# A hybrid decoder layer in split float32 on one core: memory keys in wide and narrow matmuls, a bank per 128 features, and another order of the small products around them

## The chip, the cores and the metric

One NeuronCore of a Trainium2 chip runs the whole layer as one program. The metric is the device time of one execution in microseconds, median of several runs. TensorE is called PE here (its weight loads PEld), VectorE DVE, ScalarE ACT, GpSimd POOL and SyncE SP.

## What is computed

```python
# x, mem: (1, 256, 1024) float32, one layer
proj = h @ w_in                       # qa ka va | qg kg vg rg glr
moba_o = causal softmax attention, 8 heads x 64, ALiBi     # one block of 256: plain causal
b = cumsum(log_sigmoid(glr @ w_gate_up + b_gate) / 16)     # gated linear attention, 4 heads
attn = einsum('bhtd,bhsd,bhtsd->bhts', qg, kg, exp(b_t - b_s))   # causal, chunks of 64
gla_o = rmsnorm(attn @ vg + carried state) * gla_norm_g * silu(rg)
x = LN1(alpha*x + concat(moba_o, gla_o) @ w_mix_o)
k, v = split(mem @ w_xkv)             # 4 heads x 256, 256 memory tokens
x = LN2(alpha*x + softmax((x @ w_xq) k^T / 16) v @ w_xo)
x = LN3(alpha*x + relu(x @ w_ff1)**2 @ w_ff2)
```

## The kernel before

Every large matmul is done in three parts: each float32 operand is split into a high part (rounded to `float32r`) and a low part, and hi x hi, hi x lo and lo x hi are added up in a bank of PSUM. Weights come in units of 128x2048 (half a "chunk" of 512 columns or 512 rows) into four raw buffers. ACT casts a unit to `w_hi` (`hi_half`), DVE subtracts to get `w_lo` (`lo_half`), and only then can PE use the low part and SP load the unit four places on. Both weight tensors have two places, taken by the chunk's parity. There are no queues with a scheduler: each engine's instructions stand in the order in which its block is written, and they are tied by counting semaphores. `FRONT_FILLS` says which bank each result takes and how often the bank has been filled before, `CHUNK_END` which result must be full before a chunk's weight buffer is overwritten.

The part that matters here lies between the softmax of the self attention and the mixing projection. The names in PE's program:

- `pt0` to `pt7`: transposes of the eight heads' probabilities. `rg0`, `rg1`: the gate of the linear attention. `pv0`, `pv1`: probabilities times values, four heads each. `diag`: the diagonal of the linear attention, 4 tiny float32 matmuls.
- `xk0` to `xk3`: memory keys, one bank for 256 features, made by `features`: two groups of 128 features, each 8 steps of three 128x256 matmuls (`three`). The activations (the transposed memory) are in `actB_hi` and `actB_lo`.
- `lv0` to `lv6` and `off0`, `off1`: the decayed products of the linear attention, one level for each distance 64, 32, ..., 1. For each level DVE makes exponents (`exponents`), ACT exponentiates (`decay`), POOL multiplies keys and queries by them, PE multiplies (`level`, float32, 128x128 x4), and DVE puts the result into `att` under a mask (`masked`). `off` is the product between chunks.
- `xv00`, `xv01`: memory values by `tokens` (8 steps of three 128x512 matmuls). `av0`, `av1`: `att` times the values. `mo00` to `mo11`: the mixing projection, chunk 9 and then chunk 10 by `rows`; in the last quarter of chunk 9 stand `gt0`, `gt1`, the transposes of the gated result.

Behind `av` there is a chain of engines: DVE adds the diagonal (L1090), ACT squares (L703), DVE and POOL make the scale, DVE applies it (L1103), makes the low half of chunk 10's first unit (L891), and, once ACT has copied the transposes (L651), their low parts (L1050) and the low half of the second unit. `rows(10, ...)` on PE wants the latter at its third step of 12 (k = 2). The low half of chunk 9's second unit is made by DVE ahead of `av`, from a cast that stands on ACT's list behind the two copies of `off0` and `off1` (L693).

The query projection of the cross attention, later in the kernel, already has another form (`block`, with `high` and `low`): a bank holds 128 features in two halves. One 128x512 matmul of the high weights runs over high and low activations side by side, and one 128x256 matmul of the low weights adds to the right half. The halves are added afterwards.

Of the kernel before, what the change touches and what calls it, by code (L numbers as in the profile page):

```python
# [109 lines left out]
def raw_count(u):  # L110
# [25 lines left out]
CHUNK_END = {0: "kg1", 1: "qa3", 2: "ka3", 3: "va1", 4: "vg1", 5: "rg1", 6: "xk1", 7: "xk3", 8: "xv01",  # L136
# [5 lines left out]
def build(nc, x, xT, memT, w_in, w_glr, w_gate_up, b_gate, gla_norm_g, w_mix_o, ln1_g, ln1_b, w_xq, w_xkv,  # L142
# [7 lines left out]
    with ctx:  # L150
        def sb(name, shape, dt=f32):
            return ctx.enter_context(nc.sbuf_tensor(name, shape, dt))

        def sem(name):
            return ctx.enter_context(nc.semaphore(name))
# [8 lines left out]
        actB_hi = sb("actB_hi", [P, 8, S], f32r)  # L164
        actB_lo = sb("actB_lo", [P, 8, S], f32r)
# [65 lines left out]
        lng = probs[:, 2048:3072]  # L231
        memv = probsT[:, 0:2048].rearrange("p (t n) -> p t n", t=2)
# [68 lines left out]
        mem_hi, mem_lo = sem("mem_hi"), sem("mem_lo")  # L301
# [231 lines left out]
        def _(act):  # L533
# [12 lines left out]
            def hi_half(c, half):  # L546
                hi(unit(c, half), w_hi[:, c % 2, half, :], c)
# [92 lines left out]
            for h in range(4, 8):  # L640
                transposed(h)
            hi_half(6, 1)
# [11 lines left out]
            mix(1, "pv1")  # L654
            b = wait_full(act, "diag")
            act.copy(diag[:], b[:, 0:8]).then_inc(freed("diag"), 1)
# [9 lines left out]
            def memk(n):  # L666
                evacuate(f"xk{n}", memkT[:, 2 * n:2 * n + 2, :].rearrange("p m s -> p (m s)"))
# [16 lines left out]
            decay(7)  # L684
            act.wait_ge(x_in, 16)
            for c in range(2):
                wait_out(act, f"xk{2 + c}")
                seed(bank[FILL[f"mo0{c}"][0]], 0, c)
            hi_half(9, 0)
# [22 lines left out]
            def piece(k, name=None):  # L712
                if name is None:
                    wait_full(act, "av1")
                    wait_out(act, "lv6")
                    src = mem_pieces[k]
# [163 lines left out]
        def _(dve):  # L880
# [177 lines left out]
            lo_half(6, 1)  # L1058
            silu(1)
            mix(0, "pv0")  # L1060
            mix(1, "pv1")
# [3 lines left out]
            lo_half(7, 1)  # L1065
            masked(0)
            exponents(4)
            masked(1)
            lo_half(8, 0)
            exponents(5)  # L1070
            masked(2)
            lo_half(8, 1)
            exponents(6)
            masked(3)
            exponents(7)
            masked(4)
# [251 lines left out]
        def _(pe):  # L1328
# [7 lines left out]
            def full(name):  # L1336
                return bank_full[FILL[name][0]]
# [75 lines left out]
            def high(c, dst, k, m):  # L1413

                pe.matmul(dst[:, :].rearrange("p (h s) -> p h s", h=2), weight(c, k, m * P, (m + 1) * P)[0],  # L1415
                          actA[:, :, k, :], start=k == 0, stop=False, skip_group_check=True)

            def low(c, dst, k, m):
                return pe.matmul(dst[:, S:2 * S], weight(c, k, m * P, (m + 1) * P)[1], actA_hi[:, k, :],  # L1419
                                 start=False, stop=k == 7, skip_group_check=True)  # L1420
# [90 lines left out]

            tokens(3, 0, A, "va0")
# [12 lines left out]
            for h in range(4, 8):  # L1525
                transpose_probs(h)
            tokens(5, 1, A, "rg1")
            for name in ["va0", "va1"] + [f"pt{h}" for h in range(HA)]:
                wait_out(pe, name)
            for n in range(2):  # L1530
                b = begin(f"pv{n}")
                for h in range(4 * n, 4 * n + 4):
                    r = slice(64 * (h % 2), 64 * (h % 2) + 64)
                    c = (h // 2 - 2 * n) * S
                    pe.matmul(b[r, c:c + S], va[:, 0, h * DA:(h + 1) * DA], probsT[:, h * 384:h * 384 + S],  # L1535
                              start=True, stop=False)
                    i = pe.matmul(b[r, c + P:c + S], va[:, 1, h * DA:(h + 1) * DA],
                                  probsT[:, h * 384 + S:h * 384 + 384], start=False, stop=True)
                i.then_inc(full(f"pv{n}"), 1)
            b = begin("diag")  # L1540
            pe.wait_ge(qkdiag_done, 1)
            pe.wait_ge(headsel_done, 2)
            for t in range(2):
                for f in range(2):
                    k = 4 * t + 2 * f
                    i = pe.matmul(b[:, k:k + 2], qkdiag[:, f * S + t * P:f * S + (t + 1) * P], headsel[:],
                                  start=True, stop=True)
            i.then_inc(full("diag"), 1)

# [242 lines left out]
```

## Time and profile before

| | us |
|---|---|
| median of 3 runs | 408.29 |
| range of the runs | 408.09 to 408.89 |
| profiled execution, its own time | 407.74 |
| its span, first to last instruction | 405.9 |

The page gives busy shares by engine, and the chain that ended last: followed back from the last instruction, it says in which engine's hands the time lay. A matmul's duration in the timeline overlaps that of the next, since they are pipelined; what one costs is read from the distance of starts. A float32 matmul shows as two entries (4 matmuls are "x8"), a `float32r` one as one.

### The profile page before, as it was taken

Reading aid. Unit: us, or ns where it says so; the run is one execution under the profiler, and the core shown is the slowest. Engines: PE = TensorE matmul, PEld = TensorE weight load, DVE = VectorE, ACT = ScalarE, POOL = GpSimd, SP = SyncE. Lnnn points to the kernel's source line nnn. Section 1 sums busy time; section 2 is a strip of 40 time slices with the busy share of each in tenths; the row PEclk is TensorE's granted clock in tenths of the full one; section 3 lists DMA queues with packets and bytes.
Section 4 is the critical chain, followed back from the end, with each engine's and each line's share of the span. In section 5 each row is a group of like instructions: output and inputs, shape, how many; then the busy total and the mean of one; then the engine's idle time right before and its main releaser. Section 6 shows DMA issues by size and latency. Waiting matters only on the chain.

```text
span 405.9 us, 5774 instructions
## 1 busy us (share of the span) xinstructions
PE 398.2 (98%) x2208; PEld 343.1 (85%) x2208; DVE 280.7 (69%) x364; ACT 206.3 (51%) x286; POOL 63.6 (16%) x61
## 2 busy tenths in 40 slices
PE   8999999999999999999999999999999999999993
PEld 5888888899988888899988888888888888888882
DVE  4689566998784796968658859383746475664826
ACT  6666569656264628555733466352716343444400
POOL 2039400046950105000006100000000000000000
PEclk9999999999999999999999999999999999999999
DMA  8998737635526390837265274645665637364002
GB/s 282 314 393 290 259 117 290 222 105 208 207 105 207 107 304 6 286 130 221 92 206 178 54 288 146 207 175 200 207 208 182 231 111 269 136 220 194 0 0 103
DMA packets 32364, 75.70 MB, mean 186 GB/s; under 512 B 1526, under 2 KB 3926, under 8 KB 32342
## 3 DMA queue, kind: packets, MB, share of 16 engines
q1 hardware_dynamic: 31952, 75.24, 53.6%
q10 hardware_dynamic: 390, 0.17, 0.3%
q8 instruction: 14, 0.23, 0.2%
q14 instruction: 8, 0.07, 0.0%
HBM read 74.35 MB, written 1.05 MB: 186 GB/s over the span
## 4 chain that ended last, share of the span: by engine, by line
PE 98%; DVE 1%; issue 0%; POOL 0%; DVEq 0%; POOLq 0%
PE bank L1341 20%; PE bank L1342 19%; PE bank L1343 19%; PE bank L1729 13%; PE bank L1415 8%; PE bank L1734 7%; PE bank L1419 4%; PE bank L1557 2%; PE bank L1347 1%; PE bank L1407 1%; PE bank L1509 1%; PE bank L1535 0%; PE bank L1590 0%; PE bank L1642 0%; PE bank L1501 0%; PE bank L1500 0%
## 5 line engine op out<-in xcount | busy, mean ns | idle before, releaser
L891 DVE TENSOR_TENSOR w_lo<-raw,w_hi 128x2048 fp32r<-128x2048 f32 x36 | 83.8, 2334 | 13.4 <-ACT w_hi L544 13.3
L1276 DVE TENSOR_TENSOR w_lo<-raw,w_hi 128x2048 fp32r<-128x2048 f32 x24 | 55.0, 2291 | 40.3 <-ACT w_hi L828 40.3
L544 ACT CAST w_hi<-raw 128x2048 fp32r<-128x2048 f32 x38 | 72.2, 1917 | 18.1 <-PE bank L1343 14.2
L1341 PE MATMUL bank<-w_hi,actB_hi 128*128 128x512 f32 x192 | 75.6, 394 | 0.0
L1342 PE MATMUL bank<-w_lo,actB_hi 128*128 128x512 f32 x192 | 74.8, 390 | 0.0
L1343 PE MATMUL bank<-w_hi,actB_lo 128*128 128x512 f32 x192 | 74.8, 389 | 0.0
L828 ACT CAST w_hi<-raw 128x2048 fp32r<-128x2048 f32 x24 | 46.0, 1916 | 38.2 <-PE bank L1343 38.2
L1729 PE MATMUL bank<-actA,w_hi 128*128 128x512 f32 x224 | 53.3, 390 | 0.0
L1729 PEld LDWEIGHTS bank<-actA,w_hi 128*128 128x128 f32 x224 | 41.6, 188 | 8.3
L1343 PEld LDWEIGHTS bank<-w_hi,actB_lo 128*128 128x128 f32 x192 | 36.0, 188 | 7.6
L1341 PEld LDWEIGHTS bank<-w_hi,actB_hi 128*128 128x128 f32 x192 | 36.1, 188 | 7.2
L1342 PEld LDWEIGHTS bank<-w_lo,actB_hi 128*128 128x128 f32 x192 | 36.1, 188 | 6.9
L1341 PE MATMUL bank<-w_hi,actA 128*128 128x512 f32 x96 | 38.2, 397 | 0.0
L1343 PE MATMUL bank<-w_hi,actA 128*128 128x512 f32 x96 | 37.5, 390 | 0.0
L1342 PE MATMUL bank<-w_lo,actA 128*128 128x512 f32 x96 | 37.4, 390 | 0.0
L1415 PE MATMUL bank<-actA,w_hi 128*128 128x512 f32 x144 | 35.9, 392 | 0.0
L520 POOL TENSOR_TENSOR rstd<-vareps,minus_half 128x1 f32<-128x1 f32 x6 | 3.3, 545 | 194.9 <-DVE vareps L1122 194.8
L1415 PEld LDWEIGHTS bank<-actA,w_hi 128*128 128x128 f32 x144 | 26.0, 188 | 5.4 <-issue 0.7
L1734 PEld LDWEIGHTS bank<-actA,w_lo 128*128 128x128 f32 x224 | 28.7, 191 | 1.1
L1734 PE MATMUL bank<-actA,w_lo 128*128 128x256 f32 x224 | 29.1, 283 | 0.0
L813 ACT COPY att<-bank 128x256 f32<-128x256 f32 x28 | 10.3, 377 | 34.5 <-PE bank L1734 34.5
L1341 PEld LDWEIGHTS bank<-w_hi,actA 128*128 128x128 f32 x96 | 18.0, 188 | 4.4 <-issue 0.7
(192 smaller groups left out, 617.4 us busy)
## 6 DMA issues: line engine op xcount, KB each, us to landing
raw<-in_w_ff SPq DMA_DIRECT2D x32, 1024.0 KB, 5.3
raw<-in_w_in SPq DMA_DIRECT2D x10, 1024.0 KB, 7.9
raw<-in_w_xkv SPq DMA_DIRECT2D x8, 1024.0 KB, 5.0
raw<-in_w_mix_o SPq DMA_DIRECT2D x4, 1024.0 KB, 4.9
raw<-in_w_xq SPq DMA_DIRECT2D x4, 1024.0 KB, 5.1
raw<-in_w_xo SPq DMA_DIRECT2D x4, 1024.0 KB, 4.9
raw<-in_w_in SPq DMA_DIRECT2D x4, 512.0 KB, 5.6
probs<-in_ln_g SPq DMA_DIRECT2D x3, 512.0 KB, 6.2
```

What stands on the lines that cost most here:

```text
L544: act.copy(dst, half_view(u)).then_inc(hi_done, 1)
L813: act.copy(relu[:, f, m * S:(m + 1) * S], bank[b][:, S:2 * S]).then_inc(small_done, 1)
L828: act.copy(w_hi[:, (C_LOOP + k) % 2, half, :], raw[:, u % RAW, :]).then_inc(hi_done, 1)
L891: dve.tensor_tensor(dst, half_view(u), hi_part.bitcast(f32), ALU.subtract).then_inc(lo_done, 1)
L1276: dve.tensor_tensor(w_lo[:, c % 2, half, :], raw[:, u % RAW, :], w_hi[:, c % 2, half, :].bitcast(f32), ALU.subtract).then_inc(lo_done, 1)
L1341: pe.matmul(dst, stat[0], mov[0], start=start, stop=False, skip_group_check=on)
L1342: pe.matmul(dst, stat[0], mov[1], start=False, stop=False, skip_group_check=on)
L1343: return pe.matmul(dst, stat[1], mov[0], start=False, stop=stop, skip_group_check=on)
L1415: pe.matmul(dst[:, :].rearrange("p (h s) -> p h s", h=2), weight(c, k, m * P, (m + 1) * P)[0], actA[:, :, k, :], start=k == 0, stop=False, ...
L1419: return pe.matmul(dst[:, S:2 * S], weight(c, k, m * P, (m + 1) * P)[1], actA_hi[:, k, :], start=False, stop=k == 7, skip_group_check=True)
L1729: pe.matmul(bank[m][:, :].rearrange("p (h s) -> p h s", h=2), w_hi[:, par, k // 4, a:a + P], actA[:, :, k, :], start=k == 0, stop=False, s ...
L1734: i = pe.matmul(bank[m][:, S:2 * S], w_lo[:, par, k // 4, a:a + P], actA_hi[:, k, :], start=False, stop=k == 7, skip_group_check=True)
```

## The change

The memory keys get the form of `block`: eight results `xk00` to `xk31` of 128 features, a bank each, by `high` and `low` over `actB` (now one tensor with both parts). ACT copies both halves of each bank to SBUF (`memk`, eight copies of 128x512 where there were four), and DVE adds the halves (`memk_sum`, five additions with both operands in SBUF) behind the low half of chunk 9's second unit and ahead of the diagonal. `diag` and `pv0` move ahead of `rg1`, right behind the transposes; `pv1` goes behind `xk10`. The levels are done two at a time, the last with `off`; level pairs 4, 5 and 6, `off` stand in the middle of `xv00` and `xv01`. On ACT and DVE the copies, exponents and half conversions are put in an order that follows this.

```diff
@@ FRONT_FILLS, CHUNK_END
-    + [("rg1", 3), ("pv0", 4), ("pv1", 5), ("diag", 6), ("xk0", 0), ("xk1", 1)]
-    + [("lv0", 4), ("lv1", 5), ("xk2", 2), ("lv2", 6), ("lv3", 7), ("xk3", 3), ("lv4", 4), ("lv5", 5),
-       ("xv00", 0), ("lv6", 6), ("off0", 7), ("off1", 4), ("xv01", 1), ("av0", 5), ("av1", 6)]
+    + [("diag", 0), ("pv0", 1), ("rg1", 3), ("xk00", 0), ("xk01", 1)]
+    + [("xk10", 2), ("pv1", 7), ("lv0", 4), ("lv1", 5), ("xk11", 3), ("xk20", 0), ("xk21", 1), ("xk30", 2),
+       ("lv2", 6), ("lv3", 7), ("xk31", 3),
+       ("xv00", 0), ("lv4", 4), ("lv5", 5), ("xv01", 1), ("lv6", 6), ("off0", 7), ("off1", 4), ("av0", 5), ("av1", 6)]
@@ ACT
+            def memk(h, m):
+                evacuate(f"xk{h}{m}", memk_halves[h][:, m].rearrange("p h s -> p (h s)"))
             decay(0)
             hi_half(7, 0)
             decay(1)
-            memk(0)
+            memk(0, 0)
             hi_half(7, 1)
+            memk(0, 1)
+            memk(1, 0)
+            mix(1, "pv1")
             decay(2)
             decay(3)
-            memk(1)
+            memk(1, 1)
             hi_half(8, 0)
+            memk(2, 0)
+            hi_half(8, 1)
+            memk(2, 1)
+            memk(3, 0)
             decay(4)
-            hi_half(8, 1)
-            memk(2)
             decay(5)
+            memk(3, 1)
             decay(6)
-            memk(3)
+            hi_half(9, 0)
             decay(7)
@@ DVE
             masked(6)
-            lo_half(9, 0)
             lo_half(9, 1)
+            def memk_sum(h):
+                wait_out(dve, f"xk{h}1")
+                parts = [(0, 1), (1, 2)] if h == 0 else [(0, 2)]
+                for a, b in parts:
+                    v = memk_halves[h][:, a:b]
+                    i = dve.tensor_tensor(memkT[:, 2 * h + a:2 * h + b, :], v[:, :, 0, :], v[:, :, 1, :], ALU.add)
+                    if b < 2:
+                        link(i)
+                i.then_inc(mem_sum, 1)
+            memk_sum(0)
+            for h in range(1, HX):
+                dve.wait_ge(mem_sum, h)
+                memk_sum(h)
             wait_out(dve, "diag")
@@ PE
-            features(6, 0, B, "xk0")
-            features(6, 1, B, "xk1", between=lambda: level(0))
-            level(1)
-            features(7, 0, B, "xk2", between=lambda: level(2))
-            level(3)
-            features(7, 1, B, "xk3", between=lambda: level(4))
-            level(5)
-            tokens(8, 0, B, "xv00", between={4: lambda: level(6)})
-            off()
-            tokens(8, 1, B, "xv01")
+            memory_keys(0, 0)
+            memory_keys(0, 1)
+            memory_keys(1, 0)
+            values_of(1)
+            level(0)
+            level(1)
+            memory_keys(1, 1)
+            memory_keys(2, 0)
+            memory_keys(2, 1)
+            memory_keys(3, 0)
+            level(2)
+            level(3)
+            memory_keys(3, 1)
+            tokens(8, 0, B, "xv00", between={4: levels_4_5})
+            tokens(8, 1, B, "xv01", between={4: last_level})
```

Where the order moves, first on PE around the first memory keys. Before, the second group of `xk1` (bank 1) has the first level (bank 4) between its groups:

```order
L1341 MATMUL bank1<-actB_hi,w_hi 128x256
L1342 MATMUL bank1<-actB_lo,w_hi 128x256
L1343 MATMUL bank1<-actB_hi,w_lo 128x256
L1557 MATMUL bank4<-reset,qk 128x128 [waits bank_free4,lev_done]
L1557 MATMUL bank4<-reset,qk 128x128 x3
L1341 MATMUL bank1<-actB_hi,w_hi 128x256
L1342 MATMUL bank1<-actB_lo,w_hi 128x256
L1343 MATMUL bank1<-actB_hi,w_lo 128x256
```

and now `xk10` (bank 2) is followed by `pv1` (bank 7), whose first and last rows are shown, and by the levels 0 and 1 (banks 4 and 5), and then by `xk11` (bank 3):

```order
L1439 MATMUL bank2<-actB,w_hi 128x512 [waits bank_free2]
L1439 MATMUL bank2<-actB,w_hi 128x512 x7
L1443 MATMUL bank2<-actB,w_lo 128x256 x8
L1543 MATMUL bank7<-probsT,values 64x256 [waits bank_free6,bank_free5,bank_free7,bank_free4]
...
L1545 MATMUL bank7<-probsT,values 64x128
L1586 MATMUL bank4<-reset,qk 128x128 [waits bank_free4,lev_done]
L1586 MATMUL bank4<-reset,qk 128x128 x3
L1586 MATMUL bank5<-qkdiag,qk 128x128 [waits bank_free5,lev_done]
L1586 MATMUL bank5<-qkdiag,qk 128x128 x3
L1439 MATMUL bank3<-actB,w_hi 128x512 [waits bank_free3]
L1439 MATMUL bank3<-actB,w_hi 128x512 x7
L1443 MATMUL bank3<-actB,w_lo 128x256 x8
```

Three matmuls a step have become two, one of them of 512 columns, and three small products stand together.

Second, on PE in the memory values. Before, level 6 (bank 6) stands in the middle of `xv00` (bank 0), and `off` (banks 7 and 4) between it and `xv01` (bank 1):

```order
L1342 MATMUL bank0<-w_lo,actB_hi 128x512
L1343 MATMUL bank0<-w_hi,actB_lo 128x512
L1557 MATMUL bank6<-reset,qk 128x128 [waits bank_free6,lev_done,lo_done]
L1557 MATMUL bank6<-reset,qk 128x128 x3
L1341 MATMUL bank0<-w_hi,actB_hi 128x512
...
L1343 MATMUL bank0<-w_hi,actB_lo 128x512
L1568 MATMUL bank7<-qk 128x128 [waits bank_free4,bank_free7,lev_done]
L1568 MATMUL bank4<-qk 128x128
...
L1341 MATMUL bank1<-w_hi,actB_hi 128x512 [waits bank_free1]
```

and now, in the middle of `xv01`:

```order
L1365 MATMUL bank1<-w_hi,actB 128x512
L1366 MATMUL bank1<-w_lo,actB 128x512
L1367 MATMUL bank1<-w_hi,actB 128x512
L1586 MATMUL bank6<-reset,qk 128x128 [waits bank_free6,lev_done]
L1586 MATMUL bank6<-reset,qk 128x128 x3
L1597 MATMUL bank7<-qk 128x128 [waits bank_free4,bank_free7,lev_done]
L1597 MATMUL bank4<-qk 128x128
...
L1365 MATMUL bank1<-w_hi,actB 128x512
```

So `off` has moved behind the first half of `xv01`, and only half of `xv01` is left between it and `av`.

Third, on DVE ahead of the diagonal (L1090 before, L1114 after). Before, it follows the two low halves of chunk 9:

```order
L1030 COPY_PREDICATED att<-const,bank6 128x512 [waits bank_free5,bank_full6]
L891 TENSOR_TENSOR w_lo<-raw,w_hi 128x2048 [waits hi_done] x2
L1090 SCALAR_TENSOR_TENSOR values<-values,diag,bank5 128x128 [waits bank_full6,bank_free6]
L1090 SCALAR_TENSOR_TENSOR values<-values,diag,bank5 128x128 x3
L1090 SCALAR_TENSOR_TENSOR values<-values,diag,bank6 128x128 x4
```

and now:

```order
L1040 COPY_PREDICATED att<-const,bank6 128x512 [waits bank_free5,bank_full6]
L901 TENSOR_TENSOR w_lo<-raw,w_hi 128x2048 [waits hi_done]
L1097 TENSOR_TENSOR probs<-probs 128x256 [waits bank_free1]
L1097 TENSOR_TENSOR probs<-probs 128x256 [waits dve_link]
L1097 TENSOR_TENSOR probs<-probs 128x512 [waits bank_free3,mem_sum]
L1097 TENSOR_TENSOR probs<-values 128x512 [waits bank_free1,mem_sum]
L1097 TENSOR_TENSOR probs<-probsT 128x512 [waits bank_free3,mem_sum]
L1114 SCALAR_TENSOR_TENSOR values<-values,diag,bank5 128x128 [waits bank_full6,bank_free0]
```

Five additions of the halves of the memory keys have come between the low half of the second unit and the diagonal; the first unit's low half has moved ahead of the masks.

## Rows read from the trace of the kernel before

**Rows 1.** The page: the chain that ended last, by engine.
```profile
PE 98%; DVE 1%; issue 0%; POOL 0%; DVEq 0%; POOLq 0%
```

**Rows 2.** Waits between 79 and 142 us: who waited for whom, us, times, longest.
```profile
PEld bank L1341 <- DVE w_lo L891: 0.2, 1, 0.2
```

**Rows 3.** Timeline of PE: start us, us, engine, line; a decay level among memory-key matmuls.
```profile
93.10 1.05 PE L1557 MATMUL bank<-reset,qk 128*128 128x128 f32 x8
...
94.11 0.28 PE L1342 MATMUL bank<-actB_lo,w_hi 128*128 128x256 f32 x1
...
96.87 1.05 PE L1557 MATMUL bank<-qkdiag,qk 128*128 128x128 f32 x8
```

**Rows 4.** Timeline of PE in the query projection of the cross attention.
```profile
166.34 2.00 PE L1415 MATMUL bank<-actA,w_hi 128*128 128x512 f32 x8
...
169.13 2.00 PE L1415 MATMUL bank<-actA,w_hi 128*128 128x512 f32 x8
```

**Rows 5.** Timeline of PE from the transposes to the first memory keys.
```profile
73.77 1.47 PE L1509 MATMUL bank<-const,probs 128*128 128x128 f32 x12
...
75.31 0.40 PE L1342 MATMUL bank<-w_lo,actA 128*128 128x512 f32 x1
...
80.35 0.39 PE L1343 MATMUL bank<-w_hi,actA 128*128 128x512 f32 x1
...
83.47 1.05 PE L1546 MATMUL bank<-headsel,qkdiag 128*128 128x2 f32 x8
...
84.59 0.28 PE L1342 MATMUL bank<-actB_lo,w_hi 128*128 128x256 f32 x1
```

**Rows 6.** Timeline of PE from the last decay product to the output projection.
```profile
120.28 0.39 PE L1342 MATMUL bank<-w_lo,actB_hi 128*128 128x512 f32 x1
...
125.52 1.05 PE L1590 MATMUL bank<-values,att 128*128 128x128 f32 x8
...
141.38 0.39 PE L1341 MATMUL bank<-w_hi,actA 128*128 128x512 f32 x1
```

**Rows 7.** Timeline of ACT: the copies of the last decay product and the cast behind.
```profile
120.05 0.65 ACT L693 COPY att<-bank 128x256 f32<-128x256 f32 x2
120.58 1.93 ACT L544 CAST w_hi<-raw 128x2048 fp32r<-128x2048 f32 x1
```

**Rows 8.** Timeline of DVE from the second low half of chunk 9 to that of chunk 10.
```profile
122.53 2.29 DVE L891 TENSOR_TENSOR w_lo<-raw,w_hi 128x2048 fp32r<-128x2048 f32 x1 [1.39 <-ACT w_hi L544]
128.49 2.16 DVE L1090 SCALAR_TENSOR_TENSOR values<-values,diag,bank 128x128 f32<-128x128 f32 x8 [3.66 <-PE bank L1590]
...
134.49 2.28 DVE L891 TENSOR_TENSOR w_lo<-raw,w_hi 128x2048 fp32r<-128x2048 f32 x1
137.73 1.29 DVE L1050 TENSOR_TENSOR actA<-bank,actA 128x512 fp32r<-128x512 f32 x2 [0.96 <-ACT actA L651]
138.94 2.28 DVE L891 TENSOR_TENSOR w_lo<-raw,w_hi 128x2048 fp32r<-128x2048 f32 x1
```

**Rows 9.** Timeline of DVE: element-wise operations with both operands in SBUF.
```profile
81.01 0.42 DVE L999 TENSOR_TENSOR qk<-gla 128x256 f32<-128x256 f32 x1
81.47 0.42 DVE L1000 TENSOR_TENSOR qk<-gla 128x256 f32<-128x256 f32 x1
...
163.66 2.49 DVE L1165 TENSOR_TENSOR again<-probs,again 128x512 fp32r<-128x512 f32 x4
```

**Rows 10.** Timeline of ACT: exponential of a decay level.
```profile
105.08 0.64 ACT L664 ACTIVATE qk<-qk 128x512 f32<-128x512 f32 x1
```

**Rows 11.** Timeline of POOL: products of the decay levels.
```profile
103.30 0.92 POOL L483 TENSOR_TENSOR qk<-gla,qk 128x256 f32<-128x256 f32 x1
...
108.05 1.03 POOL L483 TENSOR_TENSOR qk<-gla,qk 128x256 f32<-128x256 f32 x1
...
111.14 0.91 POOL L483 TENSOR_TENSOR qk<-gla,qk 128x256 f32<-128x256 f32 x1
```

**Rows 12.** Timeline of DVE: a low half beside the first of these levels.
```profile
105.04 2.28 DVE L891 TENSOR_TENSOR w_lo<-raw,w_hi 128x2048 fp32r<-128x2048 f32 x1
```

More of the change, by code:

```diff
@@ L134 @@
     FILL[_name] = (_bank, sum(b == _bank for b, _ in FILL.values()))
-CHUNK_END = {0: "kg1", 1: "qa3", 2: "ka3", 3: "va1", 4: "vg1", 5: "rg1", 6: "xk1", 7: "xk3", 8: "xv01",
+CHUNK_END = {0: "kg1", 1: "qa3", 2: "ka3", 3: "va1", 4: "vg1", 5: "rg1", 6: "xk11", 7: "xk31", 8: "xv01",
              10: "mo11", 11: "xv11", 12: "xq11", 13: "xq3", 15: "xo11", C_FF1_0: "hid1"}
@@ L641, in _ @@
                 transposed(h)
+            b = wait_full(act, "diag")
+            act.copy(diag[:], b[:, 0:8]).then_inc(freed("diag"), 1)
             hi_half(6, 1)
@@ L653, in _ @@
             mix(0, "pv0")
-            mix(1, "pv1")
-            b = wait_full(act, "diag")
-            act.copy(diag[:], b[:, 0:8]).then_inc(freed("diag"), 1)
             def seed(bank_at, t, c):
@@ L1058, in _ @@
             lo_half(6, 1)
+            mix(0, "pv0")
             silu(1)
-            mix(0, "pv0")
-            mix(1, "pv1")
             exponents(2)
@@ L1065, in _ @@
             lo_half(7, 1)
+            mix(1, "pv1")
             masked(0)
-            exponents(4)
             masked(1)
             lo_half(8, 0)
+            exponents(4)
+            lo_half(8, 1)
             exponents(5)
             masked(2)
-            lo_half(8, 1)
+            masked(3)
             exponents(6)
-            masked(3)
             exponents(7)
+            lo_half(9, 0)
             masked(4)
@@ L1411, in wait_hi, with high, low @@
                 pe.wait_ge(hi_done, hi_count(u))
-            def high(c, dst, k, m):
+            def high(c, dst, k, m, act=actA):
                 pe.matmul(dst[:, :].rearrange("p (h s) -> p h s", h=2), weight(c, k, m * P, (m + 1) * P)[0],
-                          actA[:, :, k, :], start=k == 0, stop=False, skip_group_check=True)
-            def low(c, dst, k, m):
-                return pe.matmul(dst[:, S:2 * S], weight(c, k, m * P, (m + 1) * P)[1], actA_hi[:, k, :],
+                          act[:, :, k, :], start=k == 0, stop=False, skip_group_check=True)
+            def low(c, dst, k, m, act=actA):
+                return pe.matmul(dst[:, S:2 * S], weight(c, k, m * P, (m + 1) * P)[1], act[:, 0, k, :],
                                  start=False, stop=k == 7, skip_group_check=True)
@@ L1510, in transpose_probs, with values_of, diagonal @@
                 i.then_inc(full(f"pt{h}"), 1)
+            def values_of(n):
+                b = begin(f"pv{n}")
+                for h in range(4 * n, 4 * n + 4):
+                    wait_out(pe, f"pt{h}")
+                for h in range(4 * n, 4 * n + 4):
+                    r = slice(64 * (h % 2), 64 * (h % 2) + 64)
+                    c = (h // 2 - 2 * n) * S
+                    pe.matmul(b[r, c:c + S], va[:, 0, h * DA:(h + 1) * DA], probsT[:, h * 384:h * 384 + S],
+                              start=True, stop=False)
+                    i = pe.matmul(b[r, c + P:c + S], va[:, 1, h * DA:(h + 1) * DA],
+                                  probsT[:, h * 384 + S:h * 384 + 384], start=False, stop=True)
+                i.then_inc(full(f"pv{n}"), 1)
+            def diagonal():
+                b = begin("diag")
+                pe.wait_ge(qkdiag_done, 1)
+                pe.wait_ge(headsel_done, 2)
+                for t in range(2):
+                    for f in range(2):
+                        k = 4 * t + 2 * f
+                        i = pe.matmul(b[:, k:k + 2], qkdiag[:, f * S + t * P:f * S + (t + 1) * P], headsel[:],
+                                      start=True, stop=True)
+                i.then_inc(full("diag"), 1)
             tokens(3, 0, A, "va0")
@@ L1526, in _ @@
                 transpose_probs(h)
+            for name in ("va0", "va1"):
+                wait_out(pe, name)
+            diagonal()
+            values_of(0)
             tokens(5, 1, A, "rg1")
[L1528 to L1548, printed above, removed]
             def level(n):
@@ L1570, in off, with memory_keys, levels_4_5, last_level @@
                             i.then_inc(full(f"off{r}"), 1)
-            features(6, 0, B, "xk0")
-            features(6, 1, B, "xk1", between=lambda: level(0))
-            level(1)
-            features(7, 0, B, "xk2", between=lambda: level(2))
-            level(3)
-            features(7, 1, B, "xk3", between=lambda: level(4))
-            level(5)
-            tokens(8, 0, B, "xv00", between={4: lambda: level(6)})
-            off()
-            tokens(8, 1, B, "xv01")
+            def memory_keys(h, m):
+                c, at = 6 + h // 2, 2 * (h % 2) + m
+                b = begin(f"xk{h}{m}")
+                for k in range(8):
+                    if at == 0 and k % 4 == 0:
+                        wait_hi(unit(c, k // 4))
+                    high(c, b, k, at, actB)
+                for k in range(8):
+                    if at == 0 and k % 4 == 0:
+                        wait_lo(pe, unit(c, k // 4))
+                    i = low(c, b, k, at, actB)
+                i.then_inc(full(f"xk{h}{m}"), 1)
+            memory_keys(0, 0)
[3 more added lines that the diff above has]
+            level(0)
+            level(1)
+            memory_keys(1, 1)
[3 more added lines that the diff above has]
+            level(2)
+            level(3)
+            memory_keys(3, 1)
+            def levels_4_5():
+                level(4)
+                level(5)
+            def last_level():
+                level(6)
+                off()
+            tokens(8, 0, B, "xv00", between={4: levels_4_5})
+            tokens(8, 1, B, "xv01", between={4: last_level})
             for name in ("vg0", "vg1", "off0", "off1", "lv6"):
```

15 lines of the change are left out of this document (8 added, 7 removed).

## The prediction

> **What bounds the kernel now.** I read the page's chain first. 98% of it lies on PE [rows 1], so a microsecond is won only where PE has less to issue and lost only where PE waits. Next I looked for waits of PE near the change, from the softmax to the mixing projection. One is listed, and it is small: PEld waits 0.2 us for a low half from DVE [rows 2]. The timelines say which one. DVE makes the low half of chunk 10's second unit from 138.94 to 141.22 [rows 8], and PE starts the matmul that wants it (k = 2 of chunk 10) at 141.38 [rows 6]. The matmuls do not halt, but the time to spare is used up: 0.16 us from the end of the low half to the matmul is the least such a hand-over takes there. The reader should keep this place in mind, since the change works on the DVE chain that leads to it. Last I read PE's starts inside the region, since durations overlap.
>
> **What PE no longer has to do.**
>
> Memory keys. A group of 8 steps with three 128x256 matmuls runs from one decay level to the next. Its second matmul starts at 94.11 and the next level at 96.87, so 23 distances are 2.76, 0.12 each, and 24 are 2.88 [rows 3]. The wide and narrow form exists in the query projection: 8 wide and 8 narrow matmuls take 169.13 - 166.34 = 2.79 [rows 4]. The columns are the same (768 a step); what goes is one start in three. Saved: 0.09 a group, 8 groups, 0.72 us.
>
> The Trainium skill ("TensorE: Matmul & The Clock Gate", Back-to-back issue gap) has a distance of N/2.4 ns plus 2.5 for isolated matmuls. By that a step would go from 327.5 to 325.0 ns, an estimate of 0.16 us for the 64 steps instead of 0.72, and the sum below would end at about +0.6 instead of 0. The trace does not agree with so small a fixed part: 0.12 against the page's 0.109 for 256 columns. So the rows decide.
>
> Fewer float32 stretches. The small products are float32 between `float32r` matmuls. 12 entries (transposes) take 75.31 - 0.23 - 73.77 = 1.31 [rows 5], 8 entries (a level) take 94.11 - 0.12 - 93.10 = 0.89 [rows 3]. The difference gives 0.105 an entry, thus 0.84 for the 8 and 0.05 for the change of kind. Before there are 10 stretches (transposes 4 to 7; `pv` and `diag`; seven levels; `off`), now 5. Saved: 5 x 0.05 = 0.25. The bounds are 0 (the moved pieces now open with several waits for banks, and each such start can cost what was won) and 0.25.
>
> Together 0.97 at most and 0.72 at least; I take 0.9.
>
> **What the moved pieces could wait for.** With the lengths above (`pv0` and `pv1` (83.47 - 80.58) / 2 = 1.45 each, `diag` 84.47 - 83.47 = 1.0, `rg1` 80.58 - 75.08 = 5.5 [rows 5]) PE's new calendar is: `diag` 75.0, `pv0` 76.0, `rg1` 77.5, `xk00` 83.0, `xk01` 85.8, `xk10` 88.6, `pv1` 91.4, levels 0 and 1 from 92.8, four groups from 94.6 to 105.7, levels 2 and 3 to 107.5, `xk31` to 110.3, half of `xv00` to 113.0, levels 4 and 5, the rest, half of `xv01` to about 120.2, level 6 and `off` to about 121.9. ACT's four additional copies I cost at nothing: it gets one bank each 2.8 us, and a copy of this size takes about 0.64 [rows 10], with one cast of a unit (120.58 to 122.53 with the hand-over [rows 7, 8]) in between. Without that room they would cost 0.64 each, 2.6 together. I find each bank free and each weight half ready by then, with one narrow place, the levels 4 and 5, which is a rival below.
>
> **What DVE gets, and why it counts.** `memk_sum` is five additions with operands in SBUF. Two of 128x256 have the distance of two dependent ones, 81.47 - 81.01 = 0.46 [rows 9]. Four independent ones of 128x512 take 2.49, so 0.60 each with 0.09 of tail; dependent ones add the tail and 0.04, 0.72 [rows 9]. Sum: 0.46 + 0.46 + 0.72 + 0.72 + 0.60 = 2.96 us. Before, DVE sat idle for 3.66 us ahead of the diagonal [rows 8], which would hide it. But the cover is gone, because `off` moved. I count from the moment E at which `off` is done on PE (120.05 before, where ACT's first copy starts [rows 7]; 120.28 - 0.23 gives the same [rows 6]).
>
> DVE's side, from E: copies of `off`, 0.53 until the cast; cast to low half 122.53 - 120.58 = 1.95 [rows 7, 8]; low half 2.20 until DVE is free (2.28 less the 0.08 by which a next one starts early, 138.94 against 137.73 + 1.29 [rows 8]). That is E + 4.68. Additions, 2.96: E + 7.64, where the diagonal starts. From there to chunk 10's first low half 134.49 - 128.49 = 6.00, the half 2.20: E + 15.84. The low parts of the transposes follow at once. Before they waited 0.96 for ACT, which was the limit there; now DVE is the later one. 1.21 for them (138.94 - 137.73), 2.28 for the second half: E + 19.33 [rows 8].
>
> PE's side, from E: before, 24 wide matmuls of `xv01` lay between E and `av`, 125.52 - 120.05 = 5.47. Now 12 do, 2.74. From `av` to the k = 2 matmul 141.38 - 125.52 = 15.86 [rows 6]. So PE wants the half for E + 18.60.
>
> The hand-over adds 0.16: E + 19.49. PE stands still for 0.89 us, less what it waits already a step earlier, for `gt1`'s low parts at the start of chunk 10 (part of the same time, not a second price). Everything after is paced by PE, so the stall ends in the total.
>
> **Sum.** -0.9 + 0.9 = 0. The profiled execution's span stays at 405.9 and its own time at 407.7; the median of the runs is 0.55 above that, so I predict 408.3. A difference under 0.2% (0.8 us) is about what a measurement of this kernel cannot tell from no change.
>
> **Rivals.**
>
> *The gain stays.* If the DVE chain is 0.9 us shorter than I count (additions in 2.1, or the copies of `off` starting earlier), PE does not wait: 408.3 - 0.9 = 407.4. For it: all my terms are taken from single rows, and the stall is the difference of two numbers near 19. Against: the 0.2 us of PEld [rows 2] says nothing is left to absorb a delay, so each tenth counts at once.
>
> *Levels 4 and 5 come late.* POOL may start level 4 only when `lv2` has been filled (106.6) and ACT has done `decay(4)`, which now stands behind the copy of `xk30` (full at 105.9). With copy and exponential at 0.64 each [rows 10] that is 107.2. A level takes POOL 4.75 (103.30 to 108.05) or 3.09 (108.05 to 111.14) [rows 11]. PE wants level 5 at 113.0 + 0.84 = 113.8. Twice 3.09 gives 113.4, in time. Twice 4.75 gives 116.7: a stall of 2.9 us, which the chain behind E does not give back, thus 411.2. It decides from 3.3 us a level on. For the slow rate: the 4.75 level had a low half of DVE beside it, with both operands in SBUF [rows 11, 12]. Against: in the new order no low half stands beside level 4 or 5 on DVE, whose next one (chunk 9) needs level 5's exponents to be over first. The Trainium skill ("SBUF — State Buffer", Who interferes with whom) gives such an operation of DVE and a reading one of POOL an exclusive lock on a shared port. By that rule the slow level is the one beside the low half, as in the rows, and levels 4 and 5 should run at the fast rate.
>
> *The additions hold more.* If dependent additions on freshly copied halves take 0.9 instead of 0.72, or PE restarts slowly, the stall is 1.4 and the time 408.8. This lies within the forecast's margin.
>
> **Numbers.** No change within 0.2% (407.5 to 409.1) gets 0.62. The gain stays (or enough of it): 0.20. Slower by over 0.2%, by the levels or by a stall over 1.7: 0.18. The likeliest time is 408.3. The range reaches down to the full gain with its upper bound, 407.3, and up to a stall of 1.9, 409.3; what is left out is mostly the late levels. The forecast's own range is 407.8 to 408.8.
>
> **What would show it.** In the changed profile the groups of memory keys should start 2.79 apart, and `av` should start 0.7 to 1.0 us earlier than 125.52. DVE should run from the low half of chunk 9 over five additions straight into the diagonal, with no idle time. PE should show one gap of 0.7 to 1.1 us within the first 6 wide matmuls of chunk 10, released by DVE's low half, and from there on stand where it stood before. The prediction is wrong if that gap is missing (then faster), or if PE waits for POOL's product ahead of level 5 (then slower), or if the groups do not get shorter.

## The result, and the profile after

Over 20 runs of each kernel the changed one takes 409.22 us (408.53 to 410.16) and the one before 408.37 (407.85 to 409.27). The ratio is 1.0019, with a 95% interval of 1.0013 to 1.0026: 0.8 us slower, just inside what I had called no change. The profiled execution took 409.61 us, its span was 407.6. I had expected 405.9. The median is inside the wide range that I gave (407.3 to 409.3), near its upper end, and outside the narrow one (407.8 to 408.8).

The page's head and its chain by engine, of the changed kernel:

```profile
span 407.6 us, 5658 instructions
...
PE 93%; DVE 3%; ACT 2%; issue 1%; POOL 0%; DVEq 0%; POOLq 0%
```

PE's share of the chain has fallen from 98% [rows 1] to 93%; DVE and ACT have come in. All waits of PE by the list of waits (the first stands at the program's start, before as now):

```profile
PE bank L1431 <- POOL reset L452: 1.5, 1, 1.5
PE bank L1365 <- DVE w_lo L901: 0.5, 1, 0.5
```

The second is new. Timeline of PE around it, at the start of chunk 10:

```profile
140.69 0.47 PE L1365 MATMUL bank<-w_hi,actA 128*128 128x512 f32 x1
...
141.91 0.39 PE L1367 MATMUL bank<-w_hi,actA 128*128 128x512 f32 x1
142.84 0.50 PE L1365 MATMUL bank<-w_hi,actA 128*128 128x512 f32 x1 [0.55 <-DVE w_lo L901]
143.18 0.39 PE L1366 MATMUL bank<-w_lo,actA 128*128 128x512 f32 x1
```

The third step's first matmul starts 0.93 after the one ahead of it, where 0.23 is usual, and released by a low half of DVE. With 0.08 extra a step before (140.69) and 0.11 in the restart (142.84 to 143.18 is 0.34, where 0.23 is usual) PE loses 0.89 us here. Next the chain that leads to it, first ACT (copies of `off`, cast), then DVE (low half of chunk 9; the five additions; the diagonal, L1114; low half of chunk 10; low parts of the transposes), the answer to [rows 7, 8]:

```profile
123.43 0.65 ACT L702 COPY att<-bank 128x256 f32<-128x256 f32 x2 [3.66 <-PE bank L1597]
123.97 1.92 ACT L549 CAST w_hi<-raw 128x2048 fp32r<-128x2048 f32 x1
```

```profile
125.92 2.29 DVE L901 TENSOR_TENSOR w_lo<-raw,w_hi 128x2048 fp32r<-128x2048 f32 x1 [1.80 <-ACT w_hi L549]
128.13 1.61 DVE L1097 TENSOR_TENSOR probs<-probs 128x256 f32<-128x256 f32 x3
129.77 0.69 DVE L1097 TENSOR_TENSOR probs<-values 128x512 f32<-128x512 f32 x1
130.50 0.69 DVE L1097 TENSOR_TENSOR probs<-probsT 128x512 f32<-128x512 f32 x1
131.10 2.15 DVE L1114 SCALAR_TENSOR_TENSOR values<-values,diag,bank 128x128 f32<-128x128 f32 x8
...
137.10 2.29 DVE L901 TENSOR_TENSOR w_lo<-raw,w_hi 128x2048 fp32r<-128x2048 f32 x1
139.30 1.28 DVE L1060 TENSOR_TENSOR actA<-bank,actA 128x512 fp32r<-128x512 f32 x2
140.50 2.28 DVE L901 TENSOR_TENSOR w_lo<-raw,w_hi 128x2048 fp32r<-128x2048 f32 x1
```

From E = 123.43 the diagonal starts 7.67 later (7.64 was counted); the low parts of the transposes start at 139.30, E + 15.87 (15.84 counted). DVE has no idle time between the low half and the diagonal. The low half that PE waits for ends at 142.78 (140.50 + 2.28), and PE's matmul stands at 142.84, 0.06 behind it; with the 0.11 of the restart that is the 0.16 that the prediction counted for the hand-over.

### The profile page after: what moved, and what is told of

Same layout as the page of the kernel before. It is cut to its first block, busy times and chain, and to the rows that moved or that the text cites. A ratio compares the mean times of both kernels' runs of the same rounds, so it can differ in the third digit from the quotient of the medians.

```text
span 407.6 us, 5658 instructions
## 1 busy us (share of the span) xinstructions
PE 399.3 (98%) x2144; PEld 340.5 (84%) x2144; DVE 280.8 (69%) x369; ACT 207.9 (51%) x290; POOL 61.2 (15%) x61
## 4 chain that ended last, share of the span: by engine, by line
PE 93%; DVE 3%; ACT 2%; issue 1%; POOL 0%; DVEq 0%; POOLq 0%
PE bank L1365 16%; PE bank L1366 16%; PE bank L1367 16%; PE bank L1786 13%; PE bank L1439 12%; PE bank L1791 7%; PE bank L1443 6%; PE bank L1586 2%; PE bank L1431 1%; ACT w_hi L549 1%; DVE w_lo L901 1%; PE bank L1371 1%; PE bank L1533 1%; ACT qk L712 1%; DVE probs L1097 1%
## 5 line engine op out<-in xcount | busy, mean ns | idle before, releaser
L1365 PE MATMUL bank<-w_hi,actB 128*128 128x512 f32 x192 | 75.6, 394 | 0.0
L1366 PE MATMUL bank<-w_lo,actB 128*128 128x512 f32 x192 | 74.8, 390 | 0.0
L1367 PE MATMUL bank<-w_hi,actB 128*128 128x512 f32 x192 | 74.8, 389 | 0.0
L1367 PEld LDWEIGHTS bank<-w_hi,actB 128*128 128x128 f32 x192 | 36.0, 188 | 7.6
L1365 PEld LDWEIGHTS bank<-w_hi,actB 128*128 128x128 f32 x192 | 36.1, 188 | 7.2
L1366 PEld LDWEIGHTS bank<-w_lo,actB 128*128 128x128 f32 x192 | 36.1, 188 | 6.8
```

The lines of the kernel that those rows point to most:

```text
L1365: pe.matmul(dst, stat[0], mov[0], start=start, stop=False, skip_group_check=on)
L1366: pe.matmul(dst, stat[0], mov[1], start=False, stop=False, skip_group_check=on)
L1367: return pe.matmul(dst, stat[1], mov[0], start=False, stop=stop, skip_group_check=on)
```

## Experiments

For most of these kernels an average over runs can tell 0.3 us at best. The profiles tell more, in two numbers. One is the distance on PE from the second four transposes (L1509 before, start 73.77 [rows 5]) to `av` (125.52 [rows 6]): 51.75 before, 51.33 after, all of the edited work of PE. The other is the rest of the span counted from those transposes: span minus their start (spans unrounded from the traces: 405.95 before, 407.56 changed). It leaves out what happens earlier, where the programs are alike, and where profiled executions differ by up to 1.4 us (last section).

| kernel | transposes to `av` | E to diagonal | PE's extra time in chunks 9 and 10 | span from transposes on, against before | runs, ratio to before (95%) |
|---|---|---|---|---|---|
| before | 51.75 | 8.44 | 0 | 0 (332.18) | |
| changed | 51.33 | 7.67 | 0.9 | +0.53 | 1.0019 (1.0013 to 1.0026) |
| additions early | 51.33 | 5.72 | 0 | -0.36 | 0.9989 (0.9975 to 1.0003) |
| cast first | 51.34 | 6.00 | 0 | -0.38 | 0.9987 (0.9974 to 1.0000) |
| keys alone | 51.56 | 8.45 | 0 | -0.16 | 0.9993 (0.9980 to 1.0007) |
| keys alone, level 5 later | 51.02 | 8.44 | 0 | -0.69 | 0.9990 (0.9982 to 0.9999) |
| values together | 50.93 | 5.72 | 0 | -0.75 | 0.9981 (0.9971 to 0.9991) |
| levels single | 51.35 | 5.72 | 0 | -0.40 | one run |
| before, five operations | 51.74 | 8.47 | 0 | +0.04 | one run |
| before, ten operations | 51.75 | 10.91 | 1.4 | +1.51 | 1.0047 (1.0030 to 1.0063) |
| changed, five more | 51.34 | 10.89 | 4.3 | +3.94 | one run |

The extra time is the sum of what distances of starts have above 0.23 for wide and 0.105 for small matmuls; the 0.08 by which PE is late whenever it goes back from small to wide ones is left out. For example 332.18 is 405.95 - 73.77. In every row the last but one column is, to about 0.1, the change in the distance plus PE's extra time.

### Additions early

```diff
@@ DVE of the changed kernel
             masked(0)
             masked(1)
+            memk_sum(0)
+            dve.wait_ge(mem_sum, 1)
+            memk_sum(1)
             lo_half(8, 0)
...
             exponents(6)
+            dve.wait_ge(mem_sum, 2)
+            memk_sum(2)
             exponents(7)
...
             masked(5)
+            dve.wait_ge(mem_sum, 3)
+            memk_sum(3)
             masked(6)
             lo_half(9, 1)
-            memk_sum(0)
-            for h in range(1, HX):
-                dve.wait_ge(mem_sum, h)
-                memk_sum(h)
```

> The changed kernel with the five additions of memory-key halves spread over idle times of DVE further up (two after the mask of level 1, one between the exponents, one ahead of the mask of level 6) instead of standing in one piece ahead of the diagonal. Theory A (the additions lie on the chain from the last decay product to the low half of chunk 10): the diagonal starts 2.9 us earlier on DVE, the gap of 0.8 us of PE in chunk 10 and its slow restart vanish, and the kernel is 0.9 us faster than the changed one, 0.4 us (0.1%) faster than the kernel before. Rival B (the gap comes from ACT's additional copies or from a late weight transfer): the gap stays, and so does the time of the changed kernel, +0.8 us against before. The distance from the second four transposes to av on PE stays at 51.3 in both.

E is 122.64 in this run. The diagonal on DVE:

```profile
128.36 2.15 DVE L1117 SCALAR_TENSOR_TENSOR values<-values,diag,bank 128x128 f32<-128x128 f32 x8 [0.95 <-PE bank L1650]
```

It follows E by 5.72 and is paced by PE again. The gap is gone, the distance on PE unchanged. The diagonal starts 1.95 earlier than in the changed kernel (7.67 - 5.72) and not 2.9, since now PE's last product for it decides and no longer DVE. Counted from the transposes the span is 331.82, 0.9 below the changed kernel's 332.70. Against before it is 0.36 lower, where the distance on PE is 0.41 lower. Theory A holds; rival B falls, since ACT's copies and the transfers are as they were.

### Cast first

```diff
@@ ACT of the changed kernel
             evacuate("xv00", memv[:, 0, 0:512])
+            hi_half(9, 1)
             for r in range(2):
                 b = wait_full(act, f"off{r}")
                 ...
-            hi_half(9, 1)
             evacuate("xv01", memv[:, 1, 0:512])
```

> The changed kernel with one edit: ACT casts the second unit of chunk 9 ahead of the two copies of off, not behind them; the additions stay where they are. Theory A: the cast starts some 4 us earlier, its low half is made right behind the mask of level 6, the additions follow, and the diagonal starts about 1.8 us earlier on DVE (5.9 us after the end of off on PE instead of 7.7); the gap of PE vanishes although no operation was removed; 0.9 us faster than the changed kernel, 0.4 us faster than before. Rival B (the additions themselves, or the transfer, are the cause wherever the cast stands): the gap stays at 0.8 us and the time at that of the changed kernel.

```profile
129.24 2.15 DVE L1114 SCALAR_TENSOR_TENSOR values<-values,diag,bank 128x128 f32<-128x128 f32 x8
```

129.24 is 6.00 after E (123.24). Again PE has no gap, again 0.9 below the changed kernel, with every addition still in place. So the additions cost time only because the cast behind `off` holds up what stands ahead of them. It takes both edits of the change (additions here, `off` behind half of `xv01`) to make the wait.

### Keys alone, twice

```diff
@@ PE: the new form of the keys; else the order before, but levels 2 to 4 one group later, so that 4 and 5 meet
             memory_keys(0, 0)
             memory_keys(0, 1)
             memory_keys(1, 0)
             level(0)
             memory_keys(1, 1)
             level(1)
             memory_keys(2, 0)
             memory_keys(2, 1)
             level(2)
             memory_keys(3, 0)
             level(3)
             memory_keys(3, 1)
             level(4)
-            level(5)                                              # first version
-            tokens(8, 0, B, "xv00", between={4: lambda: level(6)})
+            tokens(8, 0, B, "xv00", between={4: lambda: level(5)})  # second version
+            level(6)
             off()
             tokens(8, 1, B, "xv01")
```

> Only the wide and narrow form of the memory keys with its copies and additions, in the order of the kernel before: diag and both pv behind rg1, levels single (4 and 5 stand together behind the last keys), off between the two halves of the memory values. Theory A: the additions cost nothing here, since 24 wide matmuls stand between off and av (DVE is free 7.6 us after off, the last av is full at 8.4); PE saves 0.09 for each of 8 groups, so the distance from the second four transposes to av on PE is 51.75 - 0.72 = 51.0, no gap in chunk 10, time 0.7 us (0.17%) below before. Rival C (the small products cost as much in any order and the narrow form wins less than 0.72): 51.3 or more. Rival B (additions and copies delay the chain wherever they stand): a gap of 0.5 us or more in chunk 10, time as before or above.

The distance was 51.56, between the two expectations. Timeline of PE at levels 4 and 5:

```profile
110.81 1.05 PE L1587 MATMUL bank<-reset,qk 128*128 128x128 f32 x8
112.10 1.16 PE L1587 MATMUL bank<-qkdiag,qk 128*128 128x128 f32 x8 [0.24 <-POOL qkdiag L498]
```

Level 5 starts 1.29 after level 4, where 0.84 is the work by the prediction's count: 0.45 us of waiting for POOL. It comes of the order in which I had put the two levels, not of the keys' form. So the run was repeated with level 5 later.

> The keys alone once more, with level 5 moved from behind the last keys into the middle of the first memory values and level 6 ahead of off, since PE waited 0.45 us for POOL's product of level 5 in the first version. Theory: the narrow form is worth 0.64 (8 groups at 2.80 instead of 2.88), so the distance from the second four transposes to av is 51.75 - 0.64 = 51.1, with no wait of PE for POOL and no gap in chunk 10; time 0.6 to 0.65 us below before, ratio 0.9984. Rival (something else in this order costs 0.45): 51.5 and a ratio of 0.9995.

51.02, 0.73 below before; no wait for POOL. The span from the transposes on is 0.69 below before. The runs' ratio (0.9990) has that inside its interval, but at the far side. The additions stand in both versions in one piece ahead of the diagonal and cost nothing, since E is 24 wide matmuls away from `av` as before. Rival B falls a second time.

### Values together

```diff
@@ PE, from the kernel with the additions early
             diagonal()
             values_of(0)
+            values_of(1)
             tokens(5, 1, A, "rg1")
...
             memory_keys(1, 0)
-            values_of(1)
             level(0)
             level(1)
```

The copies of `pv1` on ACT and DVE move with it.

> The changed kernel with the additions early (as in the run with the gap gone) and pv1 right behind pv0, ahead of rg1, instead of behind the third group of keys. Theory S (a small product that opens a stretch or follows a wait pays 0.1 to 0.3 us, and the change made more such places): the distance from the second four transposes to av falls from 51.33 to 51.0 to 51.1; time 0.3 us below that run, about 0.7 below before. Rival T (only the number of stretches counts, 0.05 each): 51.33 as before or 51.28.

The distance is 50.93, 0.40 less for the place of one small product; and this is the fastest kernel of the study, 0.9981 (0.9971 to 0.9991) of before. Its timeline of PE: transposes, `pv0`, the first wide matmul behind `pv1`, the two levels, `av`:

```profile
75.13 1.47 PE L1536 MATMUL bank<-const,probs 128*128 128x128 f32 x12
...
77.32 0.66 PE L1546 MATMUL bank<-probsT,values 128*64 128x256 f32 x4
...
80.12 0.50 PE L1368 MATMUL bank<-w_hi,actA 128*128 128x512 f32 x1
...
94.05 1.05 PE L1590 MATMUL bank<-reset,qk 128*128 128x128 f32 x8
94.94 1.06 PE L1590 MATMUL bank<-qkdiag,qk 128*128 128x128 f32 x8
...
126.06 1.05 PE L1650 MATMUL bank<-values,att 128*128 128x128 f32 x8
```

Rival T falls. Theory S had the sign, and a smaller size (0.2 to 0.3); what it says of waits does not stand, as the section on the prediction shows. Level 0 starts 0.89 ahead of level 1 here and 1.00 in the changed kernel, where it follows `pv1`.

### Levels single

```diff
@@ PE, from the kernel with the additions early
             level(0)
-            level(1)
             memory_keys(1, 1)
+            level(1)
...
             level(2)
-            level(3)
             memory_keys(3, 1)
+            level(3)
...
-            tokens(8, 0, B, "xv00", between={4: levels_4_5})
+            tokens(8, 0, B, "xv00", between={4: lambda: level(4), 6: lambda: level(5)})
```

> The changed kernel with the additions early, and levels 1, 3 and 5 taken out of their pairs: level 1 behind xk11, level 3 behind xk31, level 5 two steps behind level 4. Theory of the prediction (0.05 us for each stretch of small products): three more stretches, the distance from the second four transposes to av rises from 51.33 to 51.48. Theory S (the pairs save nothing, since the second of a pair pays as much): 51.25 to 51.35.

51.35 against 51.33. Three more stretches cost nothing that can be read. The prediction's 0.05 a stretch is refuted.

### More operations on the chain

The same operation at the same place in both kernels; five or ten of them (`range(1)` or `range(2)`). They leave the values as they are. Waits ahead of them, which make sure that the tiles are filled, are left out here.

```diff
@@ DVE, behind the low halves of chunk 9 (before), behind the additions (changed)
+            for n in range(2):
+                for a, b in ((0, 512), (512, 1024), (1024, 1536), (0, 256), (256, 512)):
+                    v = probs[:, a:b]
+                    link(dve.tensor_tensor(v, v, v, ALU.max))
             wait_out(dve, "diag")
```

> The kernel before with five additional operations on DVE ahead of the diagonal, 3.1 us together, half the dose of the earlier run. Theory A: DVE is free 4.7 + 3.1 = 7.8 us after off, before the last av is full (8.4), so the diagonal starts 8.4 to 8.5 us after off as without them, and PE has no gap over 0.1 us in chunk 10. Rival D (any operation there delays PE): a gap of half that of ten operations, 0.5 us or more.

> The kernel before with ten additional operations on DVE at the place of the changed kernel's additions: maximum of a tile of the memory keys with itself, each waiting for the one before, 6.2 us together. Theory A, from the counted chain: DVE is free 4.7 + 6.2 = 10.9 us after off instead of 8.4, so the diagonal is 2.4 us late; 0.96 of it is absorbed where the transposes' low parts waited for ACT; PE gets a gap of 1.4 us at the start of chunk 10, and the kernel is 1.4 to 1.5 us slower than before (ratio 1.0035). Rival D (there is further room between this chain and PE): a gap under 0.7 us and a ratio of 1.0015 or less.

Five cost nothing (diagonal 8.47 after E, no gap), ten move it to 10.91, and PE's extra time is 1.4. The runs' ratio, 1.0047, is 1.9 us, and its interval (1.2 to 2.6) has the profile's 1.51 inside. The waits of PE with ten (transposes of the gated result, L1607, and chunk 10's step, L1347):

```profile
PE bank L1347 <- DVE w_lo L891: 0.5, 1, 0.5
PE bank L1607 <- DVE values L1109: 0.2, 1, 0.2
```

> The changed kernel with five more operations on DVE behind its five additions (maximum of a tile of memory keys with itself, each waiting for the one before, 3.1 us together). Theory A (the chain has no room left): all of it arrives at PE; the diagonal starts 10.7 to 10.8 us after off instead of 7.7, and the gaps of PE in the last quarter of chunk 9 and the start of chunk 10 add up to 3.8 to 3.9 us instead of 0.8. Rival D (part of it is absorbed): under 3 us of gaps.

The diagonal starts 10.89 after E. PE's wait for the transposes of the gated result, the first in that list:

```profile
PE bank L1663 <- DVE values L1132: 2.3, 1, 2.3
```

In all PE's extra time is 4.3 us, above the 3.8 to 3.9 expected. Behind the start of the program the 2.3 us are PE's only wait, and the rest has another cause: once PE has stood still for them, its granted clock is at the lower of its two levels for about 3 us. By stretches (length, busy time of PE, granted clock, DMA share, GB/s), around the eight transposes (138.91 to 140.71) and the first matmuls behind them:

```profile
139.50:142.40 2.90, 2.77 (x10) 0.50 0.00 0
142.60:145.00 2.40, 2.40 (x12) 1.00 0.68 191
```

0.50 is 1.2 GHz and 1.00 is 2.4. The eight transposes take 1.80 (138.91 to 140.71), where they take 0.79 in the changed kernel (137.08 to 137.87), and the matmuls behind them lose 0.8 more. So PE comes to the third step of chunk 10 at 145.73, when DVE's low half (143.14 to 145.42) has been ready for 0.3 us, and has no wait there. At the full clock it would have come 1.8 us sooner and waited for that half, as in the changed kernel. So the slow stretch stands in the place of a wait and adds little to it, by an estimate 0.14 (145.73 less 145.42, less 0.06 until the matmul starts and 0.11 of restart, as above).

Against the changed kernel's 0.9 the extra time rose by 3.4, and the span by 3.4 too (336.12 - 332.70). Nothing is absorbed: 3.2 us on DVE (10.89 - 7.67) arrive as 3.4 at the end.

## Why the prediction came out as it did

**The wait, by its steps.** Each was right, and the size too: additions 2.97 (131.10 - 128.13, counted 2.96), E to diagonal 7.67 (7.64), low parts of the transposes at E + 15.87 (15.84), 0.89 us lost by PE (0.89). The control with the additions early gives 0.89 on the span. The additions alone do not make the wait: with the cast moved, and with the keys alone, all five are in place and PE has no gap in chunks 9 and 10. The doses of five and ten show how much room there was before. The rival "the gain stays" is refuted for this kernel, and is true of the two where the chain is cut.

**Memory keys, 0.72 predicted.** About right. Three starts of groups in a row are 2.80, 2.79 and 2.80 apart:

```profile
74.86 1.47 PE L1533 MATMUL bank<-const,probs 128*128 128x128 f32 x12
76.17 0.95 PE L1555 MATMUL bank<-headsel,qkdiag 128*128 128x2 f32 x8
77.05 0.66 PE L1543 MATMUL bank<-probsT,values 128*64 128x256 f32 x4
...
78.55 0.50 PE L1365 MATMUL bank<-w_hi,actA 128*128 128x512 f32 x1
...
89.69 2.00 PE L1439 MATMUL bank<-actB,w_hi 128*128 128x512 f32 x8
...
92.57 0.66 PE L1543 MATMUL bank<-probsT,values 128*64 128x256 f32 x4
...
94.07 1.16 PE L1586 MATMUL bank<-reset,qk 128*128 128x128 f32 x8
95.07 1.06 PE L1586 MATMUL bank<-qkdiag,qk 128*128 128x128 f32 x8
95.88 2.08 PE L1439 MATMUL bank<-actB,w_hi 128*128 128x512 f32 x8
...
98.75 2.00 PE L1439 MATMUL bank<-actB,w_hi 128*128 128x512 f32 x8
...
101.55 2.00 PE L1439 MATMUL bank<-actB,w_hi 128*128 128x512 f32 x8
...
104.34 2.00 PE L1439 MATMUL bank<-actB,w_hi 128*128 128x512 f32 x8
...
107.14 1.05 PE L1586 MATMUL bank<-reset,qk 128*128 128x128 f32 x8
108.02 1.06 PE L1586 MATMUL bank<-qkdiag,qk 128*128 128x128 f32 x8
108.83 2.07 PE L1439 MATMUL bank<-actB,w_hi 128*128 128x512 f32 x8
...
126.19 1.05 PE L1647 MATMUL bank<-values,att 128*128 128x128 f32 x8
```

(From here `av`, 126.19 - 74.86 = 51.33, is read too.) That makes 0.08 a group, 0.64 to 0.67 for eight. The keys alone, with level 5 later, measured 0.73 on PE's distance; that order also joins level 6 to `off`.

**Fewer stretches of small products, 0.25 predicted.** This step failed, in sign. The keys alone gained 0.73 and the whole change 0.42, so the moves lost 0.3. The price of 0.05 for a change of kind was read out of two lengths, 1.31 for 12 entries and 0.89 for 8. These are 0.109 and 0.111 an entry, and can as well be a price per entry and none for the change. The levels say that it is so: in a pair level 2 takes 0.88 (107.14 to 108.02), its eight entries; alone, or second in a pair, a level takes 0.81 to the next `float32r` matmul (93.10 to 93.91, 108.02 to 108.83), and that one is 0.08 late. The sum is 0.89 in either place. Pairs gained nothing, and single levels cost nothing.

What was lost went where `pv1` moved. `pv0` and `pv1` take 1.50 each (77.05 to 78.55, 92.57 to 94.07), 3.00 in all, and 2.80 side by side in the kernel with the values together (77.32 to 80.12). `pv1` starts 0.08 late (92.57, where `xk10` is over at 89.69 + 2.80 = 92.49), and level 0 behind it takes 1.00 instead of 0.89. That is 0.20 + 0.08 + 0.11, the 0.40 that the direct test gained, to 0.01. With the 0.73 of the keys it leaves -0.33 of the measured -0.42; the rest, 0.09, was not traced.

I took such late starts for the price of several waits, in the prediction and in theory S. The traces speak against it. From the kernel before:

```profile
80.67 0.66 PE L1535 MATMUL bank<-probsT,values 128*64 128x256 f32 x4
...
93.91 0.36 PE L1341 MATMUL bank<-actB_hi,w_hi 128*128 128x256 f32 x1
...
118.98 0.39 PE L1343 MATMUL bank<-w_hi,actB_lo 128*128 128x512 f32 x1
119.30 0.71 PE L1568 MATMUL bank<-qk 64*128 64x128 f32 x8
...
125.30 0.39 PE L1343 MATMUL bank<-w_hi,actB_lo 128*128 128x512 f32 x1
```

The first pair of numbers in a row is the form of the weights. `av` opens with waits for five results and starts on time, 0.22 behind the wide matmul (125.30 to 125.52 [rows 6]); so does `diag` behind the transposes. `pv` and `off`, whose weights are 128*64 and 64*128, start 0.32 behind a wide matmul instead of 0.23 (80.35 [rows 5] to 80.67, 118.98 to 119.30). Every late start of a small product goes with such a change of the form, and the one slow level stands behind `pv1`. Counting every change to or from these forms, there are four in this part before, six in the changed kernel and four with the values together, so that 0.40 us is 0.2 for each of the two more. No run changed the form by itself, so this is what the rows agree with and not a shown cause.

**The sum.** -0.42 + 0.9 is +0.5, and the profiles say +0.53 counted from the transposes; the runs say +0.8 (0.5 to 1.1). I had -0.9 + 0.9. So the forecast of no change beyond 0.2% stood, by half a term of good luck: the loss was sized right and the gain at twice its size, and the true value lies at the edge of the band. Of the signs that I had named, the one for the gain failed: `av` was to start 0.7 to 1.0 us earlier and, counted from the transposes, starts 0.42 earlier. The low chance that I gave to slower rested on the wrong rival.

**Levels 4 and 5.** Not late, for the reason given: level 4 took POOL from 108.52 to 111.01, 2.5 us, with no low half of DVE beside it, where it took 4.75 before. That agrees with the Trainium skill's lock ("SBUF — State Buffer", Who interferes with whom), as far as one order of the two can. In the same trace level 6 has a low half of DVE beside it (from 115.47) and takes POOL 4.8 us (115.67 to 120.48). PE found each product ready. How near this rival was is shown by the keys alone, where level 5 made PE wait 0.45 us.

## What to carry to other kernels

When an operation is called hidden, count the chain that hides it from its own start, not from the idle time in the old profile: an edit elsewhere that shortens the other side (here `off` twelve matmuls nearer to `av`) takes the cover away, and a place where a weight arrives exactly when it is wanted passes on every tenth. Fewer and larger matmuls with the same columns are worth the number of starts saved, and no more (0.73 us for 64 starts here); where the small products between them stand can be worth half as much (0.40 for one), and is read from distances of starts, product by product. Two lengths do not tell a price per piece from a price per stretch when both fit. An effect of 0.1% is settled by such distances in one profile each (they repeat to 0.01 us: 51.33, 51.34, 51.34 and 51.75, 51.74, 51.75), and a dose of the suspected cost on both kernels shows how much room there is.

## What the runs showed that I had not expected

The first matmuls differ between profiled executions, ahead of anything edited. Timeline of PE, of before and then of after:

```profile
5.79 1.17 PE L1415 MATMUL bank<-actA,w_hi 128*128 128x512 f32 x4
...
7.27 1.08 PE L1415 MATMUL bank<-actA,w_hi 128*128 128x512 f32 x4
```

```profile
5.99 1.98 PE L1439 MATMUL bank<-actA,w_hi 128*128 128x512 f32 x4
...
8.29 1.09 PE L1439 MATMUL bank<-actA,w_hi 128*128 128x512 f32 x4
```

The same eight wide matmuls start 0.2 and then 1.02 us later, the first four taking 1.98 (their entry) instead of 1.17, and from there the two programs run 1.0 to 1.1 us apart up to the transposes (73.77 and 74.86). In the other runs the transposes started between 73.91 and 75.13. So 1.1 of the 1.7 us between the two profiled spans is no effect of the change. The profile's granted clock does not show a cause (1.00 in these stretches in both), and the cause stays open. Whoever compares one profile of each kernel by their spans would have taken the change for three times as bad as it is.
